# Both attentions that run between the expert picks: masks level with the scores, reciprocals two steps later, turning and weighing later, the meta columns in the shares' bank

## The chip, the cores and the metric

The kernel runs on one core of a Trainium2 chip, in fp32. The metric is the device time of one launch in microseconds. Five engines work side by side, each through its own list of instructions in order, and wait for each other on semaphores: PE (TensorE, matmuls; PEld are its weight loads), DVE (VectorE), ACT (ScalarE), POOL (GpSimd, which here issues the gathers) and SP (which here issues the loads of weights).

## The reference

Two blocks over 256 tokens of width 1024. The first is a layer of RWKV-7 time mixing and a layer of MoBA attention (with 256 tokens one block, so plain causal attention, 16 heads of 64). The second puts 16 meta tokens in front and computes

```
xr, gr, cq, ckv, kr, g_rnn, g_att = split(norm(h) @ w_in)
y_rnn = (rg_lru(conv(xr)) * gelu(gr)) @ w_rnn_out
y_att = mla_attention(...)  # 16 heads, key = 64 + 32 rotary columns, 272 keys
h = h + (sigmoid(g_rnn) * y_rnn + sigmoid(g_att) * y_att) @ w_out
h = h + peer(norm(h))       # experts
```

`peer` scores 2 x 128 keys for each of 8 heads, takes the best 16 of the 256 candidate sums, and reads for each token, head and pick a row of u and a row of v (1024 floats each) from a table of 16,384: `coef = softmax(score) * gelu(u . x)`, `out += coef * v`. With 128 tokens on the partitions that makes 2 halves x 8 heads x 16 = 256 picks, and each brings 128 rows of 8 KB, 1 MB.

## The kernel before

Tokens are cut into two halves of 128 (t = 0 and t = 1). Half 0 goes first through the whole network. At the time when its picks begin, half 1 stands at the MoBA attention; the rest of its way (the "front") is put between the picks of half 0. Picks 0 to 127 belong to half 0, picks 128 to 255 to half 1.

**A pick.** POOL issues the gather into a seat as soon as the pick that sat there before has been used (L3434). There are 7 seats for the first picks, 6 for picks 32 to 45 and 7 again up to pick 109; from pick 110 on there are more. DVE multiplies the u half of the seat with x and sums (L3390, called the dot below), and then runs a few instructions of the routing of a later head (L3274 to L3308). For a pair of picks ACT makes the gelu and the coefficient (L3219, L3223, L3228) and writes one small diagonal matrix for each (L3235). PE multiplies the diagonals with the v halves (L3095, eight records for a pair), which frees both seats.

**The front** is a generator for each engine. It yields either a number, which is paid from a credit of 2 for each pick on PE, or a name and a lag. PE notes in `g.at` at which pick each key was issued; ACT and DVE run the next piece when that pick plus the lag has come. PE stands 3 picks ahead in its count, ACT 2, DVE 0 (`SKEW`): the front's piece of pick n stands on PE before the weighted rows of pick n - 3, and on DVE, with a lag of 1, before the dot of pick n + 1. PE serves picks in pairs, so the pieces of an odd n and of n + 1 both stand before the pair that begins with n - 3. The order on each engine is therefore written out when the program is built, and nothing is chosen on the chip.

**The late pass** (MoBA, half 1) has one step for each pick from -7 to 17. Step i on PE: scores of head i (L1636), transpose of the shares of head i - 6 (L1644), and for even i >= 10 two heads weighed with V (L1656). DVE: mask and row maximum (L1865), factor (L1868), one pick later, and the reciprocal (L1874) and the division (L1875) of the head before. ACT: exponential (L1778) and the copy of the transposed shares (L1789). Both halves of the output share bank 2, so the weighing of head 8 waits until DVE has taken the first half (`late_gated(0)`, L1915).

**The steps** (MLA, half 1) are built alike, from pick 60 to 85: scores (L2172, two banks in turn), transposes (L2182), the 16 meta columns of four heads gathered into a matrix (L2462), transposed in a bank of their own (L2191) and copied (L2475), weighing (L2208, L2214) into bank 2, which DVE clears for every four heads (L2697). DVE masks (L2676) and makes the reciprocal (L2690); ACT negates the maximum (L2446), takes the exponential (L2448), divides (L2454) and copies transposed shares (L2469). Six rows of scores are kept.

Between the two passes stand the projections of half 1 (L2057 and others, "panels" of 8 matmuls, 512 KB of weights each), the convolution on DVE (L2614, L2616), and `gates_in` (L2140), which waits on PE for it:

```
            pe.wait_ge(rgw_loaded.handle, 32)
            for n in range(2):
                pe.wait_ge(convolved[1].handle, convolved[1].at(n + 1))
                gates_in(1, n)
                yield 1.0
```

## Time and profile before

| | |
|---|---|
| runs without a profile | 1435.55 us median of 3 (1432.18 to 1435.96) |
| profiled execution | 1431.92 us, its span 1430.1 us |
| granted TensorE clock, mean | 0.914 |
| busy: PE, DVE, ACT, POOL | 83%, 62%, 36%, 21% |
| moved by DMA | 426.47 MB, mean 298 GB/s |

The span is the time from the first to the last instruction; 1.8 us lie around it. Busy shares are means over stages with different limits, so they say little of any one stage. The picks run from 604 us to the end. Before that the gathers play no part.

### The profile page before, as it was taken

The numbers are of one execution on the slowest core, as the hardware profiler recorded it, in microseconds if no ns is written. First come the engines' busy times: TensorE is split into PE (matmuls) and PEld (weight loads), VectorE is DVE, ScalarE is ACT, GpSimd is POOL, SyncE is SP. The second block draws the span as 40 slices with busy tenths as digits, with TensorE's granted clock in tenths as the row PEclk, the third lists the DMA queues.
The fourth block names the chain that finished last, engine by engine and source line by source line (L and its number), as shares of the span: only waits on it lengthen the run. The fifth ranks groups of instructions, "written<-read, shape, count | busy, mean of one in ns | idle before, by whom it ended". The sixth has DMA issues, their size and how long they took to land.

```text
span 1430.1 us, 23324 instructions
## 1 busy us (share of the span) xinstructions
PE 1183.0 (83%) x8780; PEld 798.2 (56%) x8780; DVE 884.5 (62%) x2297; ACT 515.9 (36%) x1538; POOL 294.7 (21%) x277
## 2 busy tenths in 40 slices
PE   7999998999999999986888987888766676576554
PEld 4446788986689989852666864457433222222111
DVE  7527876546534541588556636765369787777654
ACT  1215223121431530244334534842253434344334
POOL 0000000000000000124221213332253444444440
PEclk9999999999999999968989999999978867878777
DMA  8444100343566867868998999899999999999996
GB/s 311 155 155 134 33 4 3 118 147 122 191 228 226 293 236 249 299 279 351 417 383 327 409 388 418 314 398 421 418 424 424 423 426 424 426 426 424 425 426 254
DMA packets 85984, 426.47 MB, mean 298 GB/s; under 512 B 11183, under 2 KB 15663, under 8 KB 52657
## 3 DMA queue, kind: packets, MB, share of 16 engines
q0 software_dynamic: 38304, 273.70, 46.5%
q1 hardware_dynamic: 47426, 151.03, 29.3%
q8 instruction: 70, 1.15, 0.3%
q14 instruction: 40, 0.33, 0.1%
q10 hardware_dynamic: 144, 0.26, 0.0%
HBM read 421.80 MB, written 3.15 MB: 297 GB/s over the span
## 4 chain that ended last, share of the span: by engine, by line
PE 45%; DMA 27%; DVE 8%; ACT 4%; issue 3%; POOL 2%; POOLq 0%; DVEq 0%; ACTq 0%
DMA cst<-peer_in,arena 16%; PE bank L2057 13%; PE bank L3095 6%; DMA ring<-stream_in 5%; DMA arena<-peer_in,arena 5%; PE bank L1441 3%; PE bank L1528 2%; PE bank L1494 2%; DVE arena L3390 2%; PE bank L847 2%; PE bank L646 1%; PE bank L656 1%; PE bank L2982 1%; DVE cst L3390 1%; PE bank L1671 1%
## 5 line engine op out<-in xcount | busy, mean ns | idle before, releaser
L3095 PE MATMUL bank<-arena 128*64 128x512 f32 x808 | 268.5, 751 | 132.7 <-ACT arena L3235 132.7
L3390 DVE CUSTOM_DVE_ANT_0 arena<-arena 128x1024 f32<-128x1024 f32 x202 | 246.2, 1224 | 140.5 <-DMA arena<-peer_in,arena 137.7
L3434 POOL DMA_INDIRECT arena<-peer_in,arena x202 | 226.2, 1120 | 422.5 <-PE bank L3095 353.6
L2057 PE MATMUL bank<-arena,ring 128*128 128x128 f32 (+1 forms) x2112 | 249.6, 278 | 16.2 <-DMA ring<-stream_in 15.5
L2057 PEld LDWEIGHTS bank<-arena,ring 128*128 128x128 f32 x2112 | 242.2, 192 | 31.9 <-issue 23.1
L3095 PEld LDWEIGHTS bank<-arena 128*64 128x64 f32 x808 | 68.1, 160 | 269.0 <-issue 265.2
L3219 ACT ACTIVATE arena<-arena 128x2 f32<-128x2 f32 (+1 forms) x130 | 26.4, 203 | 390.5 <-DVE arena L3390 390.5
L3095 PE MATMUL bank<-row,arena 128*64 128x512 f32 x112 | 65.1, 712 | 28.3 <-ACT arena L3235 28.2
L3228 ACT ACTIVATE arena<-arena 128x1 f32<-128x1 f32 x256 | 84.2, 375 | 8.3 <-DVE arena L3396 7.5
L3223 ACT ACTIVATE arena<-arena 128x1 f32<-128x1 f32 x256 | 85.4, 380 | 4.3
L2982 PEld LDWEIGHTS bank<-arena,ring 128*128 128x128 f32 x512 | 62.8, 201 | 27.5 <-issue 27.5
L3235 ACT ACTIVATE arena<-cst,arena 128x64 f32<-128x64 f32 x256 | 76.3, 334 | 0.2
L3095 PE MATMUL bank<-cst,arena 128*64 128x512 f32 x104 | 66.3, 772 | 5.3 <-ACT arena L3235 5.3
L2982 PE MATMUL bank<-arena,ring 128*128 128x128 f32 x512 | 67.9, 289 | 0.0
L497 PE MATMUL bank<-ring,arena 128*128 128x512 f32 x128 | 55.1, 592 | 0.0
L1948 POOL DMA_DIRECT2D spill<-arena x2 | 1.1, 536 | 249.1 <-DVE arena L1839 249.1
L1441 PE MATMUL bank<-arena,ring 128*128 128x256 f32 x224 | 49.5, 379 | 0.0
L1441 PEld LDWEIGHTS bank<-arena,ring 128*128 128x128 f32 x224 | 42.5, 190 | 8.3 <-issue 2.9
L3390 DVE CUSTOM_DVE_ANT_0 cst<-cst,arena 128x1024 f32<-128x1024 f32 x26 | 31.9, 1225 | 24.4 <-DMA cst<-peer_in,arena 24.3
L3095 PEld LDWEIGHTS bank<-row,arena 128*64 128x64 f32 x112 | 14.8, 152 | 55.9 <-issue 55.6
L1826 DVE RECIPROCAL arena<-arena 128x512 f32<-128x512 f32 x8 | 26.8, 3353 | 29.6 <-ACT arena L1725 29.6
L3434 POOL DMA_INDIRECT row<-peer_in,arena x28 | 30.9, 1103 | 68.2 <-PE bank L3095 64.5
(412 smaller groups left out, 1870.2 us busy)
## 6 DMA issues: line engine op xcount, KB each, us to landing
ring<-stream_in SPq DMA_DIRECT2D x255, 512.0 KB, 5.9
ring<-stream_in SPq DMA_DIRECT2D x16, 384.0 KB, 8.2
arena<-peer_in,arena POOLq DMA_INDIRECT x202, 20.5
row<-rows_in SPq DMA_DIRECT2D x4, 512.0 KB, 18.4
spill<-arena POOLq DMA_DIRECT2D x4, 512.0 KB, 5.5
cst<-rg_w_in SPq DMA_DIRECT2D x2, 1024.0 KB, 8.6
ring<-stream_in SPq DMA_DIRECT2D x16, 128.0 KB, 4.1
arena<-spill POOLq DMA_DIRECT2D x4, 512.0 KB, 7.7
```

What stands on the lines that cost most here:

```text
L497: mm = nc.tensor.matmul(banks[t][:, :], mix[name][:, k, t * P:(t + 1) * P], slot[:, i * 512:(i + 1) * 512], start=k == 0, stop=k == KT - 1)
L847: mm = nc.tensor.matmul(bank, slot[:, k * P:(k + 1) * P], kT[:, k, t * P:(t + 1) * P], start=k == 0, stop=k == KT - 1)
L1441: mm = nc.tensor.matmul(bank[:, (m % 2) * T:(m % 2 + 1) * T], slot[:, k * P:(k + 1) * P], src[:, k, :], start=k == 0, stop=k == KT - 1)
L1494: mm = nc.tensor.matmul(core.banks[core.bank_at["vb", t, half][0]][:, :], xn["kb"][:, k, t * P:(t + 1) * P], slot[:, i * 512:(i + 1) * 512 ...
L2057: mm = nc.tensor.matmul(bank[:, at:at + width], slot[:, first + k * cols:first + (k + 1) * cols], src[:, k, :], start=k == 0, stop=k == kt ...
L2982: mm = nc.tensor.matmul(bank[:, i * P:(i + 1) * P], slot[:, k * P:(k + 1) * P], n2[t][:, k, :], start=k == 0, stop=k == KT - 1)
L3095: return nc.tensor.matmul(core.banks[2 * t + b][rows_of(j), :], diag[i % ND], places[seat[i]][:, D + b * 512:D + (b + 1) * 512], start=Fal ...
L3223: nc.scalar.activation(act_out[:, i:i + 1], act_out[:, i:i + 1], ACT.Tanh, bias=steep, scale=steep).then_inc(*activated.up())
L3228: nc.scalar.activation(act_out[:, i:i + 1], act_out[:, i:i + 1], ACT.Identity, bias=share, scale=share).then_inc(*coef_ready.up())
L3235: nc.scalar.activation(diag[i % ND], cst("halves"), ACT.Copy, scale=act_out[:, i:i + 1])\
L3390: ins = nc.vector.tensor_tensor_reduce(out=row, in0=row, in1=X2[t][i % 2], scale=STEEP, scalar=0.0, op0=ALU.mult, op1=ALU.add, accum_out=d ...
L3434: pool.indirect_dma_start(out=places[seat[i]], out_offset=None, in_=g.names["peer"], in_offset=bass.IndirectOffsetOnAxis(ap=index[:, i:i + ...
```

## The change

In the late pass DVE masks a head at the pick at which PE issues its scores (lag 0 where it was 1) and does the reciprocal and the division 3 steps after the mask where it was 1, so two steps later against the masks and one pick later in the program. ACT copies transposed shares one step later. `late_gated(0)` stays at step 16, which lag 0 puts one pick earlier. The output projection waits 3 picks after the last step where it waited 4; as each later piece of the front hangs on the one before, all of the front behind it stands one pick earlier.

In the steps the masks get lag 0 as well (`q2` gets lag 2 where it had 1, so the rotations stay where they were), reciprocals come 3 steps after the mask where it was 1, ACT divides 5 steps after the scores where it was 3 and copies shares 8 after where it was 6; PE turns 7 after where it was 6 and weighs 11 after where it was 10. Eight rows of scores are kept where it was six. The meta columns are transposed into the third quarter of the bank of the fourth head's shares and no longer into a bank of their own, so that `turn_meta`, its claim and its wait go; ACT still copies them by an instruction of their own.

```diff
@@ moba, PE and ACT
-            yield ("late", H + 8), 4
+            yield ("late", H + 8), 3
...
-                if 6 <= i < H + 6:
-                    late_keep(i - 6)
+                if 7 <= i < H + 7:
+                    late_keep(i - 7)
@@ moba, DVE
             for i in range(H + 9):
-                yield ("late", i), 1
+                yield ("late", i), 0
                 if i < H:
                     mask(i, 1)
-                if 1 <= i < H + 1:
-                    divide(i - 1, 1)
+                if 3 <= i < H + 3:
+                    divide(i - 3, 1)
                 if i == 16:
                     late_gated(0)
@@ second_mix
-    HELD, ROWS = (H, 4), (H, 6)
+    HELD, ROWS = (H, 4), (H, 8)
...
+        if t and n >= 6:
+            return LOW[:, (n - 6) * S:(n - 5) * S]
@@ second_mix, PE
+            if t and h % 4 == 3:
+                pe.wait_ge(meta_laid[t].handle, meta_laid[t].at(h + 1))
+                mm = nc.tensor.transpose(bank[:, 2 * P:3 * P], META_P[t][h // 4 % 2], cst("ident"))
...
-                if 6 <= i < H + 6:
-                    turn(i - 6, 1, 6 + i % 2)
-                if 6 <= i < H + 6 and (i - 6) % 4 == 3:
-                    turn_meta((i - 6) // 4, 1, 4)
-                if i >= 10 and i % 2 == 0:
-                    weigh((i - 10) // 2, 1, 2)
+                if 7 <= i < H + 7:
+                    turn(i - 7, 1, 6 + (i - 7) % 2)
+                if i >= 11 and i % 2:
+                    weigh((i - 11) // 2, 1, 2)
@@ second_mix, ACT
-                if 6 <= i < H + 6:
-                    keep(i - 6, 1)
+                if 8 <= i < H + 8:
+                    keep(i - 8, 1)
                 if 2 <= i < H + 2:
                     exps(i - 2, 1)
-                if 3 <= i < H + 3:
-                    divide(i - 3, 1)
-                    lay_meta(i - 3, 1)
+                if 5 <= i < H + 5:
+                    divide(i - 5, 1)
+                    lay_meta(i - 5, 1)
@@ second_mix, DVE
-                yield ("q2", n, 1), 1
+                yield ("q2", n, 1), 2
...
-                yield ("step", i), 1
+                yield ("step", i), 0
                 if i < H:
                     mask(i, 1)
-                if 1 <= i < H + 1:
-                    divide(i - 1, 1)
-                if i >= 12 and i % 4 == 0:
-                    keep_out((i - 12) // 4, 1)
+                if 3 <= i < H + 3:
+                    divide(i - 3, 1)
+                if i >= 13 and i % 4 == 1:
+                    keep_out((i - 13) // 4, 1)
```

The lines of the changed kernel lie 10 further down around the picks (the dot is L3400 for L3390, the weighted rows L3105 for L3095) and 2 further at the projections (L2059, L2142).

**First place, DVE at the end of the late pass**, around picks 9 and 10. L1874 and L1875 are reciprocal and division, L1915 is `late_gated`, the large ISA row of L3390 is the dot of a pick. Before:

```order
L3396 TENSOR_TENSOR arena<-arena 128x2
L3274 MAX arena<-arena 128x8
L3276 MAX_INDEX arena<-arena 128x8
L3277 MATCH_REPLACE cst<-arena 128x128
L3279 MAX arena<-cst 128x8
L3281 MAX_INDEX arena<-arena,cst 128x8
L3289 CAST arena<-arena 128x16
L3274 MAX arena<-arena 128x8
L1874 RECIPROCAL small<-small 128x1
L1875 TENSOR_SCALAR arena<-arena,small 128x256
L1915 TENSOR_TENSOR arena<-bank,arena 128x512
L3390 ISA arena<-arena 128x1024
```

and of the changed kernel, where the two dots shown first and last are those of picks 8 and 9:

```order
L3400 ISA arena<-arena 128x1024
L3400 ISA arena 128x1
L1874 RECIPROCAL small<-small 128x1
L1875 TENSOR_SCALAR arena<-arena,small 128x256
L1915 TENSOR_TENSOR arena<-bank,arena 128x512
L3400 ISA arena<-arena 128x1024
L3400 ISA arena 128x1
L3406 TENSOR_TENSOR arena<-arena 128x2
L3284 MAX arena<-arena 128x8
L3286 MAX_INDEX arena<-arena 128x8
```

The reading of bank 2 (L1915) stood before the dot of pick 10, behind the routing pieces of the pair 8 and 9; now it stands before the dot of pick 9, ahead of them.

**Second place, PE at `gates_in`** (L2140, changed kernel L2142), between the weighted rows of picks 30 to 37. The rows with `row` in them are those of picks 32 and 33, the x4 behind them picks 34 and 35. Before:

```order
L3095 MATMUL bank<-arena 64x512
L3095 MATMUL bank<-row,arena 64x512
L2057 MATMUL bank<-arena,ring 128x128 x32
L3095 MATMUL bank<-arena 64x512 x4
L2982 MATMUL bank<-arena,ring 128x128 x8
L2140 MATMUL bank<-arena,cst 128x128 x16
L2079 MATMUL bank<-arena,ring 128x128 x8
L2057 MATMUL bank<-arena,ring 128x128 x8
L3095 MATMUL bank<-arena 64x512 x4
```

and of the changed kernel:

```order
L3105 MATMUL bank<-arena 64x512
L3105 MATMUL bank<-row,arena 64x512
L2059 MATMUL bank<-arena,ring 128x128 x16
L2142 MATMUL bank<-arena,cst 128x128 x16
L3105 MATMUL bank<-arena 64x512 x4
L2992 MATMUL bank<-arena,ring 128x128 x8
L2081 MATMUL bank<-arena,ring 128x128 x8
L2059 MATMUL bank<-arena,ring 128x128 x24
L3105 MATMUL bank<-arena 64x512 x4
```

`gates_in` stood behind the weighted rows of picks 34 and 35 and before those of 36 and 37; now it stands before those of 34 and 35.

**Third place, DVE at the convolution** that `gates_in` waits for (L2614 and L2616; changed kernel L2624 and L2626). The dot with `row` in it is that of pick 39. Before:

```order
L3390 ISA arena 128x1
L2614 TENSOR_SCALAR arena<-arena,vec 128x128 x4
L2616 SCALAR_TENSOR_TENSOR arena<-arena,vec 128x128 x4
L3390 ISA row,arena<-row,arena 128x1024
L3390 ISA arena 128x1
L3396 TENSOR_TENSOR arena<-arena 128x2
L3274 MAX arena<-cst 128x8
L3276 MAX_INDEX arena<-arena,cst 128x8
L3277 MATCH_REPLACE cst<-arena,cst 128x256
L3279 MAX arena<-cst 128x8
L2616 SCALAR_TENSOR_TENSOR arena<-arena,vec 128x128 x8
L3390 ISA arena<-arena 128x1024
```

and of the changed kernel:

```order
L2624 TENSOR_SCALAR arena<-arena,vec 128x128 x4
L2626 SCALAR_TENSOR_TENSOR arena<-arena,vec 128x128 x4
L3400 ISA arena<-arena 128x1024
L3400 ISA arena 128x1
L2626 SCALAR_TENSOR_TENSOR arena<-arena,vec 128x128 x8
L3400 ISA row,arena<-row,arena 128x1024
L3400 ISA arena 128x1
L3406 TENSOR_TENSOR arena<-arena 128x2
L3284 MAX arena<-cst 128x8
L3286 MAX_INDEX arena<-arena,cst 128x8
L3287 MATCH_REPLACE cst<-arena,cst 128x256
L3289 MAX arena<-cst 128x8
```

The last eight convolution instructions stood between the dots of picks 39 and 40; now they stand between those of 38 and 39, one pick earlier, while PE waits for them two picks earlier.

## Rows read from the trace of the kernel before

**Rows 1.** The page: span, then DMA share and GB/s in 40 slices.

```profile
span 1430.1 us, 23324 instructions
...
DMA  8444100343566867868998999899999999999996
GB/s 311 155 155 134 33 4 3 118 147 122 191 228 226 293 236 249 299 279 351 417 383 327 409 388 418 314 398 421 418 424 424 423 426 424 426 426 424 425 426 254
```

**Rows 2.** Busy us of each engine by stretch, clock, DMA share, GB/s.

```profile
core 0: us, PE busy (x) PEld busy (x) DVE busy (x) ACT busy (x) POOL busy (x), PEclk, DMA share, GB/s
610.00:680.00 70.00, 52.76 (x256) 28.01 (x255) 59.35 (x199) 30.71 (x113) 21.04 (x18) 0.77 0.79 313
680.00:870.00 190.00, 167.32 (x1201) 131.53 (x1198) 111.22 (x306) 74.75 (x207) 45.06 (x39) 0.95 0.96 386
870.00:950.00 80.00, 59.61 (x340) 33.89 (x339) 56.30 (x181) 52.30 (x194) 29.84 (x26) 0.89 0.92 363
950.00:1060.00 110.00, 85.80 (x604) 60.86 (x603) 56.87 (x144) 38.42 (x125) 36.74 (x36) 0.92 1.02 421
1060.00:1430.10 370.10, 232.43 (x832) 83.96 (x832) 273.90 (x736) 153.03 (x548) 147.22 (x134) 0.79 0.97 408
```

**Rows 3.** Waits from 604 to 674 us: total, times, longest.

```profile
ACT arena L1789 <- PE bank L1656: 11.1, 5, 4.9
...
DVE small L1874 <- ACT arena L1778: 7.2, 8, 1.8
...
PE bank L1636 <- DVE small L1865: 6.4, 6, 1.9
PE bank L1656 <- DVE arena L1915: 5.3, 1, 5.3
```

**Rows 4.** The same columns as rows 2, two slices of the late pass.

```profile
620.00:630.00 10.00, 8.38 (x27) 4.34 (x28) 7.87 (x33) 3.64 (x13) 0.00 (x0) 0.50 0.41 172
...
660.00:670.00 10.00, 8.73 (x66) 5.15 (x64) 9.17 (x26) 3.97 (x16) 6.70 (x5) 1.00 0.71 270
```

**Rows 5.** Waits from 870 to 950 us.

```profile
PE bank L2172 <- DVE small L2676: 12.6, 8, 3.5
...
DVE small L2690 <- ACT arena L2448: 11.7, 14, 2.0
...
PE bank L2208 <- DVE arena L2697: 3.3, 3, 2.4
```

**Rows 6.** DVE in order of time: the dots of picks 64 and 78.

```profile
889.23 1.21 DVE L3390 CUSTOM_DVE_ANT_0 arena<-arena 128x1024 f32<-128x1024 f32 x1
...
934.53 1.22 DVE L3390 CUSTOM_DVE_ANT_0 arena<-arena 128x1024 f32<-128x1024 f32 x1
```

**Rows 7.** ACT in order of time: first instruction of two pairs, one after the other.

```profile
906.40 0.20 ACT L3219 ACTIVATE arena<-arena 128x2 f32<-128x2 f32 x1 [0.69 <-DVE arena L3390]
...
912.79 0.20 ACT L3219 ACTIVATE arena<-arena 128x2 f32<-128x2 f32 x1 [0.68 <-DVE arena L3390]
```

**Rows 8.** PE in order of time: picks 34 and 35, gates, picks 36 and 37, four panels.

```profile
753.49 1.94 PE L3095 MATMUL bank<-arena 128*64 128x512 f32 x8
755.36 2.05 PE L2982 MATMUL bank<-arena,ring 128*128 128x128 f32 x16
757.25 1.95 PE L2140 MATMUL bank<-arena,cst 128*128 128x128 f32 x16
765.50 3.46 PE L2140 MATMUL bank<-arena,cst 128*128 128x128 f32 x16 [6.30 <-DVE arena L2616]
...
772.47 1.94 PE L3095 MATMUL bank<-arena 128*64 128x512 f32 x8
...
774.33 7.41 PE L2057 MATMUL bank<-arena,ring 128*128 128x128 f32 x64
```

**Rows 9.** DVE in order of time: dot of pick 38, convolution pieces.

```profile
756.08 1.23 DVE L3390 CUSTOM_DVE_ANT_0 arena<-arena 128x1024 f32<-128x1024 f32 x1 [1.23 <-DMA arena<-peer_in,arena]
...
763.13 2.31 DVE L2616 SCALAR_TENSOR_TENSOR arena<-arena,vec 128x128 f32<-128x128 f32 x8
```

**Rows 10.** The same columns as rows 2, around the gates.

```profile
760.00:770.00 10.00, 4.50 (x27) 4.50 (x28) 7.63 (x24) 6.08 (x23) 0.00 (x0) 0.66 0.69 289
770.00:780.00 10.00, 10.00 (x81) 8.50 (x80) 5.28 (x16) 6.10 (x14) 2.10 (x2) 1.00 0.66 215
```

**Rows 11.** ACT in order of time: a load of a function table.

```profile
720.33 1.28 ACT L3223 ACT_TABLE_LOAD   x1
721.63 0.67 ACT L3223 ACTIVATE arena<-arena 128x1 f32<-128x1 f32 x2
```

More of the change, by code:

```diff
@@ L2211, in weigh @@
             if j % 2:
-                copied(pe, ("pm_c", n, t))
+                if t == 0:
+                    copied(pe, ("pm_c", n, t))
                 for i in range(2):
@@ L2459, in lay_meta @@
             if n >= 2 and h % 4 == 0:
-                filled(act, ("pm_c", n - 2, t))
+                filled(act, ("pt_c", 4 * n - 5, t) if t else ("pm_c", n - 2, t))
             to = META_P[t][n % 2].rearrange("p (d h w) -> p d h w", d=2, w=NM)[:, :, h % 4, :]
@@ L2468, in keep @@
                 act.wait_ge(weighed_out[t].handle, weighed_out[t].at((h - HELD[t]) // 2 + 1))
-            nc.scalar.activation(PT[t][:, at:at + width], bank[:, 0:width], ACT.Copy).then_inc(*free(("pt_c", h, t)))
+            ins = nc.scalar.activation(PT[t][:, at:at + width], bank[:, 0:width], ACT.Copy)
+            if t == 0:
+                ins.then_inc(*free(("pt_c", h, t)))
             if h % 4 == 3:
                 n = h // 4
-                bank = filled(act, ("pm_c", n, t))
+                meta = bank[:, 2 * P:3 * P] if t else filled(act, ("pm_c", n, t))[:, 0:P]
                 if n >= len(PM[t]):
                     filled(act, ("o_c", n - len(PM[t]), t))
-                nc.scalar.activation(PM[t][n % len(PM[t])], bank[:, 0:P], ACT.Copy).then_inc(*free(("pm_c", n, t)))
+                ins = nc.scalar.activation(PM[t][n % len(PM[t])], meta, ACT.Copy)
+                if t == 0:
+                    ins.then_inc(*free(("pm_c", n, t)))
+            if t:
+                ins.then_inc(*free(("pt_c", h, t)))
         def open_attended(t, n):
```

## The prediction

> **What bounds the kernel now.** I read the page first, then a table of stretches, then in each stretch the waits, and last single instructions in order of time. The page's slices of DMA share and GB/s [rows 1] show where the end is decided: from the 20th slice on the DMA engines move some 400 GB/s, and in the last 15 slices nearly always more than 414, so the picks of half 1 wait for bytes. The stretches say the same in numbers: share 1.02 from 950 to 1060 us, 0.97 from there to the end, where the last microseconds move nothing [rows 2]. The bytes are fixed, 426 MB, and the change moves none. So the change is worth what it takes from, or adds to, the time in which DMA stands idle before 950 us. Taking 1.02 as full, that idle time is (1.02 - 0.79) x 70 = 16 us in the late pass, (1.02 - 0.96) x 190 = 11 us in the projections, and (1.02 - 0.92) x 80 = 8 us in the steps [rows 2].
>
> Why is DMA idle there? A gather leaves only when a seat is free, and a seat is freed by the weighted rows on PE, which come behind a dot on DVE, a chain on ACT and whatever of the front stands ahead of them. In the late pass DVE is busy 59.35 of 70 us [rows 2], the most of any engine that the loop needs, and 7.2 us of its idle time stand ahead of the reciprocal, which waits for the exponential of the head masked just before [rows 3]. Behind the waiting reciprocal are queued the division, the next dot and so the next seat. PE has one wait of 5.3 us, for the reading of bank 2 by `late_gated`, just ahead of the weighted rows of picks 8 and 9 [rows 3]; DMA falls to 0.71 in the slice in which these end late [rows 4].
>
> In the steps DVE waits 11.7 us in 14 parts for exponentials [rows 5]. The two engines hand each other the work: the dot of an odd pick starts ACT's chain, behind that chain stands the next exponential, behind the exponential the reciprocal, and behind it the next dot. From the dot of pick 64 to that of pick 78 there are seven pairs in 45.3 us, 6.47 us a pair [rows 6]. ACT's own work in a pair is 912.79 - 906.40 = 6.39 us less an idle 0.68 us, that is 5.71 us [rows 7].
>
> **The change part by part.**
>
> *Late pass, masks and reciprocals.* No instruction is added or taken. The mask of a head comes one pick earlier, its reciprocal one pick later, and the exponential between them stays: two picks lie between where one did. The wait of 7.2 us [rows 3] goes but for remnants; its next owner is DVE's own work. The masks could now wait for PE. PE issues the scores three picks ahead, and from 620 to 630 us it works at the lower of its two clocks, 1.2 GHz (granted 0.50), busy 8.38 of 10 us [rows 4]: there PE can't follow a faster DVE, and of the 7.2 us I leave about 2.2 to it. PE's 6.4 us of waits for a mask [rows 3] shrink with it, being the same time seen from the other side. Gain 5.0 us; bounds: 0 (all goes to PE at 1.2 GHz) and 7.2.
>
> *Late pass, bank 2 and copies.* `late_gated` stands ahead of the dot of pick 9 and no longer of pick 10, so PE's 5.3 us [rows 3] lose at least a dot and the routing pieces behind it. ACT's copy, which waited 11.1 us for PE [rows 3], comes one pick later, when PE is past it. Both are parts of the same loop and I count them as cover for the 5.0 us, not beside it. Without them the gain would stop at about 7.2 - 5.3 = 2 us.
>
> *Steps.* The exponential comes one pick earlier on ACT and the reciprocal stays where it was. The ping-pong is cut, and what is late next is ACT with 5.71 us a pair. At that pace seven pairs save 7 x (6.47 - 5.71) = 5.3 us. The 12.6 us for which PE waits for masks [rows 5] go along with it. ACT gets no less work, except the wait for the meta bank, and its copies stretch over two more steps, so I take 3.5 us. Bounds: 0, and the stretch's 8 us of idle DMA. `turn_meta`'s own bank and wait go; the transposed matrix still costs one transpose and one copy: 0. Two more rows of scores lie in memory that is free by then: 0; if it were not, a mask would wait for a copy. Reading bank 2 one pick earlier takes the 3.3 us of L2208 [rows 5], which is inside the 3.5.
>
> *Projections, one pick earlier.* Here the change isn't only a shift. Since PE serves pairs, `gates_in` moves from ahead of picks 36 and 37 to ahead of 34 and 35, two picks, while the convolution that it waits for moves by one, from behind the dot of pick 39 to behind that of pick 38. Before, PE waited 6.30 us [rows 8]. Now the weighted rows of 34 and 35 (753.49 before [rows 8]) stand behind that wait. Pick 38 can only come after picks 32 and 33 free their seats, so its dot stays near 756.08 + 1.23 us; then 2.31 us of convolution [rows 9], about 760, and 3.46 us for the second gates [rows 8], about 763.5. Those weighted rows so end near 765.5, ten microseconds late. Behind them come 2.05 us of a query and 7.41 us of four panels [rows 8]: picks 36 and 37 start at 775.0 where they started at 772.47, 2.5 us late. DMA was already idle there, at 0.69 and 0.66 [rows 10], so the delay of picks 34 and 35 replaces a hole with an earlier one, and I count the 2.5 us as loss. Bounds: -1.2 us (PE has then done two panels more, 3.7 us by half of 7.41) and +10.
>
> *Table loads.* ACT loads one function table less, since two pieces that need a square root now follow each other. A load takes 1.28 us and the next activation begins right behind it [rows 11]. ACT waits for dots in the projections, so: 0, at best 1.28 us. The Trainium skill, ScalarE: Activation LUTs, section What ACT_TABLE_LOAD costs, gives about 1283 ns for the load and another 1380 ns of drain, 2.66 us in all; by it the sum would be 1.4 us lower at most. The load's duration agrees with the row, and the row shows no drain behind it.
>
> *The rest one pick earlier* is worth nothing: from 950 us DMA is full [rows 2].
>
> Sum: -5.0 - 3.5 + 2.5 = -6.0 us. Against the profiled execution, 1431.92 us, that is 1425.9. The median of the three plain runs is 3.6 us above that execution, so I put it at 1435.5 - 6.0 = 1429.5 us.
>
> **Rivals.**
> - *Both loops shorten, the gates cost a little* (forecast): 1424 to 1434 us. Chance 0.50.
> - *Given back.* The late pass gains 3 us and the steps 1.5, because landing gathers become the wait, and the gates cost 4.5. For it: DMA share is already 0.96 and 0.92 in the two later stretches [rows 2], so little room is left. Against it: no dot of the late pass waits for DMA among its larger waits [rows 3]. Time 1435.5. Chance 0.26. The Trainium skill, Trainium Kernel Development and Optimization, section Key Constraints, says that transfers of all queues run on the same 16 engines and interleave; by it an earlier gather only takes the turn of a weight panel. The trace agrees where the share is 1.02 and not in the late pass.
> - *Slower, by the gates.* The weighted rows of picks 34 and 35 stand behind a dot that needs the only seats just refilled, and all six run empty. If the hole in DMA grows by the whole ten microseconds and the two loops give 5 together, the time is 1435.5 + 10 - 5 = 1440.5. It decides from a loss of 8.5 us on. Against it: most of that hole is there already [rows 10]. Chance 0.12.
> - *More.* The late pass gives 7.2, the steps 5.3 and the gates -1.2: 13.7 us, 1422. For it: DVE's waits are 7.2 and 11.7 us [rows 3, 5]. Against it: 1.2 GHz on PE, and ACT. Chance 0.12.
>
> **How the numbers follow.** About 0.3% (4.3 us) is what a measurement of this kernel tells from no change. Below 1431.2 lie 0.43 of the forecast and all of the last case: faster 0.55. Within: 0.07 and 0.22 of the second case, 0.29. Slower: 0.12 and 0.04, 0.16. The range 1420 to 1438 leaves out the far end of the last case, 0.05, and most of the slower one with a tail of the second, 0.13. The forecast's own range is 1424 to 1434.
>
> **What would show it.** Right, if DVE's idle time ahead of the late reciprocal falls under 2 us, the share from 610 us to the end of the late pass rises above 0.83, the steps take 6 us a pair with hardly a wait at L2690's successor, and PE's long wait at the gates stands ahead of picks 34 and 35. Wrong, if masks wait for PE in the place of the reciprocals, if dots begin to wait for landings so that the pair stays at 6.4 us, or if picks 36 and 37 start more than 8 us behind their place.

## The result, and the profile after

The changed kernel takes **1419.37 us** (median of 4 runs, 1416.69 to 1421.12) against 1433.87 for the kernel before on the same chip (4 runs, 1431.59 to 1435.96): ratio **0.9898, interval 0.987 to 0.9925**, faster by 14.5 us. A second comparison, e9_after below, gave 0.9882. The forecast had -6.0 us and 1429.5; its range ended at 1420. The sign was right, the forecast size less than half of the measured one.

The profiled execution of the changed kernel took 1421.12 us, the slowest of its four, so the two traces differ by 10.8 us where the medians differ by 14.5.

The page, with the same rows as [rows 1]:

```profile
span 1419.3 us, 23316 instructions
...
DMA  8443100343556876879998999899999999999995
GB/s 308 155 156 141 34 3 3 120 141 127 193 195 229 301 256 229 296 294 403 421 421 337 418 365 423 340 381 419 422 424 424 423 424 426 426 425 426 425 425 242
```

The stretches of [rows 2], now of the changed kernel:

```profile
core 0: us, PE busy (x) PEld busy (x) DVE busy (x) ACT busy (x) POOL busy (x), PEclk, DMA share, GB/s
610.00:680.00 70.00, 61.50 (x346) 36.91 (x345) 63.22 (x219) 32.43 (x123) 21.72 (x20) 0.84 0.88 356
680.00:870.00 190.00, 164.86 (x1146) 127.14 (x1144) 111.54 (x302) 73.86 (x209) 43.36 (x40) 0.93 0.97 394
870.00:950.00 80.00, 63.18 (x376) 36.44 (x373) 60.38 (x192) 53.35 (x199) 26.89 (x25) 0.90 0.94 369
950.00:1060.00 110.00, 86.94 (x582) 58.75 (x581) 58.67 (x153) 37.78 (x124) 42.85 (x39) 0.91 1.02 421
```

The reader is to see the second last number: 0.79 to 0.88, 0.96 to 0.97, 0.92 to 0.94. Taking 1.02 as full again, DMA idles (1.02 - 0.88) x 70 + (1.02 - 0.97) x 190 + (1.02 - 0.94) x 80 = 25.7 us, where it was 35: 9 us less, nearly the 10.8 us between the traces. A share has two digits, which leaves some 2 us open on either side; within that the way the prediction kept its books holds.

The waits of the late pass, 604 to 674 us (compare [rows 3]):

```profile
PE bank L1644 <- ACT arena L1789: 5.1, 4, 2.4
...
DVE arena L1865 <- PE bank L1636: 2.1, 3, 1.3
...
PE bank L1636 <- DVE small L1865: 1.9, 1, 1.9
```

DVE's 7.2 us ahead of the late reciprocal are gone altogether. Masks now wait 2.1 us for PE, and PE waits 5.1 us for ACT's copies.

The waits of the steps, 861 to 941 us (compare [rows 5]; L2686 is the mask, L2174 the scores, L2184 the turn of a head's shares, L2473 their copy):

```profile
PE bank L2174 <- DVE small L2686: 7.8, 3, 5.0
DVE row L3400 <- DMA row<-peer_in,arena: 7.5, 2, 5.5
DVE arena L3400 <- DMA arena<-peer_in,arena: 6.0, 6, 2.4
PE bank L2184 <- ACT arena L2473: 6.0, 7, 1.5
```

And the dots of picks 64 and 78 (compare [rows 6]):

```profile
878.02 1.23 DVE L3400 CUSTOM_DVE_ANT_0 arena<-arena 128x1024 f32<-128x1024 f32 x1 [0.33 <-DMA arena<-peer_in,arena]
...
918.12 1.23 DVE L3400 CUSTOM_DVE_ANT_0 arena<-arena 128x1024 f32<-128x1024 f32 x1 [0.45 <-DMA arena<-peer_in,arena]
```

Seven pairs in 40.1 us, 5.73 us a pair, where it was 6.47. No reciprocal waits for an exponential any more; most of what DVE waits for are landings: the two rows above and 2.0 us for seats in `cst`, 15.5 us together, where it was 11.1 us from 870 to 950 us before.

The gates on PE (compare [rows 8]), and the stretch around them:

```profile
739.69 2.02 PE L2142 MATMUL bank<-arena,cst 128*128 128x128 f32 x16 [0.94 <-issue]
748.48 3.78 PE L2142 MATMUL bank<-arena,cst 128*128 128x128 f32 x16 [6.76 <-DVE arena L2626]
752.19 1.94 PE L3105 MATMUL bank<-arena 128*64 128x512 f32 x8
```
```profile
750.00:760.00 10.00, 10.00 (x72) 8.39 (x72) 4.81 (x16) 8.00 (x21) 2.83 (x2) 0.89 0.44 161
```

The weighted rows of picks 34 and 35 stand behind the wait, as forecast. So all four signs that the prediction had named for being right were there, and its sum was still far too small: they tell where the gain comes from and not how large it is.

The next table is worked out from the traces: the start of the weighted rows of a pick, less that of the kernel before, in us. The kernels of the columns are those of the experiments.

| pick | changed | e1_shift | e3_late | e4_steps | e2_noshift | e10_bank | e13_own | e17 |
|---|---|---|---|---|---|---|---|---|
| 0 | -5.0 | +1.2 | -5.1 | +7.5 | -3.5 | +0.6 | -2.9 | -6.1 |
| 16 | -5.7 | +9.0 | -7.3 | +7.2 | -5.8 | +1.1 | -2.8 | -6.7 |
| 34 | -1.3 | +11.5 | -7.4 | +6.6 | -7.9 | +0.6 | +0.6 | -7.0 |
| 36 | -9.3 | +4.7 | -6.8 | +7.8 | -6.5 | +2.3 | -7.3 | -11.8 |
| 54 | -11.8 | +2.5 | -4.3 | +9.7 | -5.8 | +4.2 | -9.8 | -13.1 |
| 78 | -14.3 | +8.0 | -6.6 | +2.4 | -12.8 | 0.0 | -5.4 | -19.0 |
| 84 | -5.4 | +15.4 | -6.6 | +2.4 | -12.7 | +0.1 | +1.0 | -19.0 |
| 104 | -13.6 | +6.5 | -6.9 | +0.3 | -17.8 | -0.8 | -7.9 | -22.1 |
| 254 | -11.9 | +9.2 | -6.1 | +0.3 | -14.3 | +0.1 | -5.3 | -20.3 |

A column is one execution. The +7.5 at pick 0 of e4_steps arose before any pick, and its time (1433.39 us) was 8 us over the highest of its six others; what that column tells is the fall from +9.7 to +0.3 behind it.

### The profile page after: what moved, and what is told of

Its sections match the earlier page's. It is cut to its first block, busy times and chain, and to the rows that moved or that the text cites. A ratio compares the mean times of both kernels' runs of the same rounds, so it can differ in the third digit from the quotient of the medians.

```text
span 1419.3 us, 23316 instructions
## 1 busy us (share of the span) xinstructions
PE 1181.3 (83%) x8780; PEld 797.2 (56%) x8780; DVE 885.3 (62%) x2297; ACT 513.6 (36%) x1537; POOL 291.2 (21%) x277
## 4 chain that ended last, share of the span: by engine, by line
PE 46%; DMA 24%; DVE 11%; ACT 4%; issue 3%; POOL 2%; POOLq 0%; DVEq 0%; ACTq 0%
PE bank L2059 14%; DMA arena<-peer_in,arena 13%; DMA cst<-peer_in,arena 9%; PE bank L3105 7%; PE bank L1441 3%; DVE arena L3400 3%; DMA ring<-stream_in 2%; PE bank L1528 2%; PE bank L1494 2%; PE bank L847 2%; PE bank L2992 2%; PE bank L646 1%; PE bank L656 1%; PE bank L1671 1%; PE bank L1574 1%
## 5 line engine op out<-in xcount | busy, mean ns | idle before, releaser
L3105 PE MATMUL bank<-arena 128*64 128x512 f32 x808 | 266.5, 745 | 132.3 <-ACT arena L3245 132.3
L3400 DVE CUSTOM_DVE_ANT_0 arena<-arena 128x1024 f32<-128x1024 f32 x202 | 246.3, 1224 | 141.3 <-DMA arena<-peer_in,arena 138.4
L3444 POOL DMA_INDIRECT arena<-peer_in,arena x202 | 223.0, 1104 | 419.4 <-PE bank L3105 349.5
L2059 PEld LDWEIGHTS bank<-arena,ring 128*128 128x128 f32 x2112 | 242.9, 192 | 17.8 <-issue 14.5
L2059 PE MATMUL bank<-arena,ring 128*128 128x128 f32 (+1 forms) x2112 | 248.6, 278 | 1.5 <-DMA ring<-stream_in 0.8
L3105 PEld LDWEIGHTS bank<-arena 128*64 128x64 f32 x808 | 67.2, 157 | 268.1 <-issue 265.1
L3105 PE MATMUL bank<-row,arena 128*64 128x512 f32 x112 | 69.2, 751 | 31.3 <-ACT arena L3245 31.3
L3105 PE MATMUL bank<-cst,arena 128*64 128x512 f32 x104 | 63.7, 745 | 0.3 <-ACT arena L3245 0.3
L3400 DVE CUSTOM_DVE_ANT_0 cst<-cst,arena 128x1024 f32<-128x1024 f32 x26 | 31.8, 1224 | 29.2 <-DMA cst<-peer_in,arena 29.1
L3400 DVE CUSTOM_DVE_ANT_0 row<-row,arena 128x1024 f32<-128x1024 f32 x28 | 34.3, 1224 | 24.9 <-DMA row<-peer_in,arena 24.6
L3105 PEld LDWEIGHTS bank<-row,arena 128*64 128x64 f32 x112 | 15.8, 162 | 58.8 <-issue 58.3
```

The lines of the kernel that those rows point to most:

```text
L2059: mm = nc.tensor.matmul(bank[:, at:at + width], slot[:, first + k * cols:first + (k + 1) * cols], src[:, k, :], start=k == 0, stop=k == kt ...
L3105: return nc.tensor.matmul(core.banks[2 * t + b][rows_of(j), :], diag[i % ND], places[seat[i]][:, D + b * 512:D + (b + 1) * 512], start=Fal ...
L3400: ins = nc.vector.tensor_tensor_reduce(out=row, in0=row, in1=X2[t][i % 2], scale=STEEP, scalar=0.0, op0=ALU.mult, op1=ALU.add, accum_out=d ...
L3444: pool.indirect_dma_start(out=places[seat[i]], out_offset=None, in_=g.names["peer"], in_offset=bass.IndirectOffsetOnAxis(ap=index[:, i:i + ...
```

## The experiments

All times are beside the kernel before on the same chip, whose median was between 1433.1 and 1435.5 us in the five groups of runs. Intervals are of the ratio and span 2 to 6 us to either side; gains given in us below are the difference of the two medians of one group.

| run | what it is | ratio, interval | us |
|---|---|---|---|
| e1_shift | before + shift | 1.0042, 1.002 to 1.0064 | 1438.98 |
| e3_late | before + late pass | 0.9945, 0.9927 to 0.9964 | 1425.53 |
| e4_steps | before + steps | 0.9921, 0.9892 to 0.995 | 1423.15 |
| e2_noshift, e18_noshift | changed, without shift | 0.9915 and 0.9905 | 1421.40, 1421.16 |
| e5_q2 | before + rotations a pick later | 0.9981, 0.9957 to 1.0005 | 1431.11 |
| e6_noq2 | before + steps, rotations as before | 0.9929, 0.9903 to 0.9955 | 1424.93 |
| e7_ownbank | before + steps, meta bank kept | 0.9968, 0.9949 to 0.9987 | 1429.89 |
| e10_bank | before + shared bank | 0.9974, 0.9946 to 1.0002 | 1430.89 |
| e9_after | changed, again | 0.9882, 0.9844 to 0.9921 | 1420.25 |
| e11_recip | changed, reciprocals 2 steps behind | 0.992, 0.989 to 0.995 | 1424.23 |
| e13_own | changed, meta bank kept | 0.9953, 0.9937 to 0.9969 | 1426.78 |
| e15_gated | changed, `late_gated` a pick later | 0.9901, 0.9874 to 0.9928 | 1420.99 |
| e8_conv, e14_conv | changed, convolutions earlier | 0.9878 and 0.9896 | 1415.16, 1418.84 |
| e12_conv2 | changed, all four taps earlier | 0.9879, 0.9841 to 0.9918 | 1420.29 |
| e16, e17_conv_noshift | e14 without shift | 0.9862 and 0.9869 | 1414.11, 1415.14 |

**The change in three parts.** The shift alone, the late pass alone and the steps alone, each laid on the kernel before, and the whole without the shift. The late pass and the steps are the hunks of the diff above for them; with the steps go the rotations two picks behind, which the shift needs as well. The shift is one number:

```
-            yield ("late", H + 8), 4
+            yield ("late", H + 8), 3
```

> The kernel before, with only the output projection waiting 3 picks for 4 after the late pass, so that all of the front behind it stands one pick earlier (and the rotations of the queries keep their place by a lag of 2). Theory A (placement): the shift pays by itself, because the first two panels of the output projection fill a wait of PE ahead of picks 16 and 17 and the rest follows; less 2 us for the gates. Expected 3 to 5 us under the kernel before, ratio 0.997. Theory B (as in the prediction): the shift only costs what the gates cost, 2.5 us over the kernel before, ratio 1.002.

> The changed kernel with the output projection put back to a wait of 4 picks: every part of the change but the shift. Theory A: 3 to 5 us slower than the changed kernel, about 10 us under the kernel before, ratio 0.993, and gates_in stands behind picks 34 and 35 again. Theory B: 2.5 us faster than the changed kernel, about 17 under the kernel before, ratio 0.988.

> The kernel before with the late pass of the changed one alone (masks level with the scores, reciprocals three steps after, copies one step later), no shift and the old steps. Both theories: DVE's wait ahead of the late reciprocal nearly gone, picks 16 and 17 used 6 to 7 us earlier than before. A: of these 6 us are left at the end, ratio 0.996. Rival: the late pass explains most of the 14.5 us by itself, ratio 0.992 or less.

> The kernel before with the steps of the changed one alone (masks, reciprocals, copies, turning, weighing, eight rows, meta columns in the shares' bank, rotations with a lag of 2), no shift and the old late pass. Both theories: 2 to 3.5 us under the kernel before, ratio 0.998, the pair of picks at about 6 us for 6.47. Rival (given back): the steps end earlier, the gathers land no earlier and the time is that of before, ratio 1.000.

Measured: +5.5 us, -12.0, -7.9 and -10.3. A theory that the shift itself pays falls: alone it costs. The three parts add to -12.7 us, and the whole gave -14.5 and -15.2. Late pass and steps together without the shift gave -12, less than the -18.2 of their sum: perhaps some of the one gain is had in place of the other, but with 3 to 4 us to either side of each of the three numbers, that isn't shown.

In e3_late the late pass alone shows this:

```profile
610.00:680.00 70.00, 54.76 (x314) 31.97 (x313) 64.89 (x221) 33.54 (x125) 20.19 (x20) 0.89 0.92 365
```
```profile
DVE arena L1865 <- PE bank L1636: 1.1, 3, 0.6
DVE small L1874 <- ACT arena L1778: 0.2, 1, 0.2
```

The first fence is the stretch of the late pass with the columns of [rows 2], the second all that DVE waited for from 604 to 674 us: 7.2 us of waiting for exponentials became 0.2, and no more than 1.1 came back as masks that wait for PE. The DMA share rose from 0.79 to 0.92.

**What in the steps pays?** They gave 10 us where I had put 3.5. First the rotations: alone, and taken out of the steps' part.

```
             for n in range(4):
-                yield ("q2", n, 1), 1
+                yield ("q2", n, 1), 2
                 rotate_queries(1, n)
```

> The kernel before with one number changed: the four rotations of the second queries (rotate_queries(n, 1)) stand on DVE two picks behind the piece of PE that they read, not one. The steps' part of the change alone took about 10 us off (0.9921), where the prediction had 3.5 and nothing for the rotations. Theory Q: about half of that comes from here, because DVE no longer stands 12.7 us ahead of the dot of pick 56, waiting for ACT's copy of the turned queries; then this kernel takes 3 to 6 us off, ratio 0.996 to 0.998. Theory P, that the cut hand-over between DVE and ACT in the steps carries the whole: 0 to 1 us, ratio 0.999 to 1.001, since the gain of the dot of pick 56 frees no seat sooner.

> The steps' part of the change alone, as in the run e4_steps, but with the rotations left where the kernel before has them (one pick behind). Theory P (the hand-over between DVE and ACT): still 8 to 10 us off, ratio 0.993 to 0.9945, and pairs of picks 64 to 78 at 6 us or below. Theory Q (the rotations): 4 to 6 us off, ratio 0.9955 to 0.997.

Measured: -3.6 us with an interval that holds no change, and -9.8 without them. The steps' gain is the same with and without within the measurement, so theory Q falls as the main cause. The pace that theory P expected, 6 us a pair or below, is missed in the trace of e6_noq2: 6.49. That execution is the highest of its seven (1437.81 us, 13 over the median), and 4.1 us of it are one wait of DVE ahead of the dot of pick 78; up to pick 76 it is 6.17, where the kernel before has 6.69 and e4_steps 5.74. So the pace there is cut by less than P said. In the trace of e5_q2 the dot of pick 56 comes 15.1 us sooner and its weighted rows 0.7 us later: a dot that is early frees no seat by itself.

Then the bank. `turn_meta` gets its own bank back, once in the new order of the steps, and the shared bank is tried in the old order.

```
                     turn(i - 7, 1, 6 + (i - 7) % 2)
+                    if (i - 7) % 4 == 3:
+                        turn_meta((i - 7) // 4, 1, 5)
...
-            if t and h % 4 == 3:
-                pe.wait_ge(meta_laid[t].handle, meta_laid[t].at(h + 1))
-                mm = nc.tensor.transpose(bank[:, 2 * P:3 * P], META_P[t][h // 4 % 2], cst("ident"))
```

> The steps' part of the change alone, as in e4_steps, but the meta columns are still turned into a bank of their own (a bank of the scores, as before, now the other one of the two) by their own piece, and copied and freed as before. If the shared bank is worth nothing, as the prediction has it: the same as e4_steps, ratio 0.990 to 0.994. Rival: PE's wait for a scores' bank that both a mask and a copy must leave is part of the steps' gain; then 3 us or more are missing, ratio 0.9945 or above.

> The kernel before, with one thing of the steps' part alone: the meta columns are turned in the bank of the shares and copied with them, in the old order of the steps. The run with a bank of their own in the new order (e7_ownbank) missed about half of the steps' gain. Theory: the bank matters only in the new order, where the copy that frees a scores' bank comes a step later; in the old one PE waits 0.7 us for it, so 0 to 1 us here, ratio 0.999 to 1.001. Rival: the shared bank gains by itself what was missing, 4 to 6 us, ratio 0.996 to 0.9975.

> The changed kernel with the meta columns of the steps turned into a bank of their own again (the other of the two scores' banks), by their own piece, copied and freed as before; all else as changed. Theory B: the shared bank is about half of the steps' gain in the new order, since PE's next scores otherwise wait for the copy that frees the scores' bank (9.7 us of such waits on the matmuls and their loads together when the steps' part ran with a bank of its own): 4 to 6 us of the gain are lost, ratio 0.992 to 0.994. Rival, the prediction's own price of nothing: 0.988 to 0.990.

Measured: -4.8 us in e7_ownbank, where e4_steps had -10.3; -4.6 in e10_bank with an interval that just holds no change; and in e13_own -7.8 us, so that undoing the bank in the changed kernel loses about 7 us, with intervals that stand apart (0.9937 to 0.9969 against 0.987 to 0.9925). The price of nothing is refuted, for the new order. For the old order the median of e10_bank lies where the rival put it (0.9974) and not where my theory did. Its trace says the same, if read like the column of e4_steps: 4.2 us behind the kernel before at pick 54, level from pick 78 on, so 4.2 us gained between. The shared bank may thus be worth some 4 us in the old order too, where PE waited 0.7 us for the copy and 1.9 us ahead of `turn_meta`; with no change still in the interval, that stays open. Both runs with a bank of their own use the other of the two scores' banks, at a place in the new order that was chosen for them; another place, or a free bank, was not tried. PE's waits in e13_own, 861 to 941 us (L2477 is the copy of the turned meta columns there, L2678 the mask):

```profile
PE bank L2174 <- ACT arena L2477: 10.1, 2, 5.1
PE bank L2174 <- DVE small L2678: 7.8, 3, 4.8
```

The changed kernel has the second row (7.8 us) and not the first. In its place it has 4.4 us for the same copy at the weighing (L2213 behind L2481), ahead of the weighted rows of picks 80 and 81, and all of PE's waits from 861 to 941 us come to 21.7 us against 23.1: the price of the bank is read from the times, not from the 10.1 us. The meta columns stood in a bank of the scores. A step after them PE wants that bank for the next scores, and ACT's copy, which frees it, now comes a step later in the order. In the table e13_own is 2.1 us behind the changed kernel at pick 0, 2.0 at pick 54, and 8.9 at pick 78. Its pair from pick 64 to 78 takes 7.00 us, that of e7_ownbank 6.35 and that of e4_steps 5.94, where the changed kernel has 5.73. These are single executions, and e6_noq2 has 6.49 with the bank shared, so a pace alone doesn't show what the bank is worth.

Two parts of the steps' change were not run alone: the eight rows of scores and the later copies.

**How far must the reciprocal stand behind?** Two steps and not three, in both loops:

```
-                if 3 <= i < H + 3:
-                    divide(i - 3, 1)
+                if 2 <= i < H + 2:
+                    divide(i - 2, 1)
```

> The changed kernel with the reciprocals of both attentions two steps behind the masks and not three, so that each stands at the dot where it stood before the change, relative to its head; all else as changed. Theory P (the gain is that of the cut hand-over): the masks alone already open one pick of room, but the exponential's chain again ends last in some steps; DVE waits 5 us or more for exponentials again over both loops, and 4 to 8 us of the gain are lost, ratio 0.992 to 0.996. Rival: one pick of room is enough, and the third step is worth nothing: 0.989 to 0.991, with hardly a wait.

Measured: 0.992, 4.0 us above e9_after in the same group of runs. DVE's waits in the steps (861 to 941 us), then in the late pass (604 to 674 us):

```profile
DVE small L2700 <- ACT arena L2452: 8.2, 12, 2.0
```
```profile
DVE small L1874 <- ACT arena L1778: 2.5, 3, 1.8
```

10.7 of the 18.9 us of [rows 3, 5] are back. The intervals of the two runs overlap (0.989 to 0.995, 0.9844 to 0.9921), so the waits are shown and their price of 4 us is likely.

**Is the earlier `late_gated` what lets the late pass gain?**

```
-                if i == 16:
+                if i == 17:
                     late_gated(0)
```

> The changed kernel with late_gated(0) a pick later on DVE, ahead of pick 10 and not of pick 9, where it stood before the change. The prediction counted its earlier place as cover for the 5.0 us of the late pass, without which the gain there would stop at about 2 us. If so, PE's wait for the reading of bank 2 grows back to some 4 us and 3 us or more of the whole gain are lost: ratio 0.991 to 0.993. Rival: the late pass gains by the cut hand-over alone, and later the delay of picks 8 and 9 is made up: 0.988 to 0.990.

Measured: 0.9901, 1420.99 us, where the rival put it; the interval (0.9874 to 0.9928) doesn't exclude a loss of 3 us. PE waits for the reading of bank 2 again, but for little, and not for the 4 us that were expected:

```profile
PE bank L1656 <- DVE arena L1915: 1.3, 1, 1.3
```

**The gates and the shift.** The convolutions of half 1 a pick earlier, with the shift and without, and once all four taps together:

```
-                yield ("xr", part, 1), 3
+                yield ("xr", part, 1), 2
                 convolve(1, part, 0)
                 convolve(1, part, 1)
-                yield ("xr", part, 1), 4
+                yield ("xr", part, 1), 3
```

> The changed kernel with the convolutions of half 1 one pick earlier on DVE (two and three picks behind their piece, not three and four), so that PE's gates meet a convolution that is done, or nearly. In the changed kernel the weighted rows of picks 34 and 35 come about 10 us late there, and the DMA share is 0.44 in the 10 us around it. If that hole costs bytes (the prediction's loss of 2.5 us, or more): 3 to 6 us faster than the changed kernel, ratio to the kernel before 0.986 to 0.988. Rival: the hole is only moved, since the seats run empty a little later at the next wait, and the time is that of the changed kernel, 0.989 to 0.991. A convolution that is earlier can also make DVE wait for PE and hold back a dot: then 0.992 or above.

> The changed kernel once more, unaltered, beside the runs below on the same chip. If the first comparison holds, 0.987 to 0.9925 of the kernel before; the sum of the parts run one by one (-7.9 us for the late pass, -10.3 for the steps, +5.5 for the shift: -12.7 us, 0.991) lies in the same interval, so a result there would say that the parts simply add. Below 0.986 or above 0.993 they would not.

> The changed kernel with the convolutions of half 1 earlier still: all four taps of a part two picks behind its piece. With three of them a pick earlier (e8_conv) the time was 0.9878, 3.2 us of PE's wait at the gates were left, and DVE's last taps stood behind a dot and its routing pieces. If those 3.2 us still cost: another 1 to 3 us, ratio 0.986 to 0.988. Rival: the block of 4.6 us on DVE holds up a dot and gives it back: 0.988 to 0.990.

> The changed kernel with the convolutions of half 1 a pick earlier, the same kernel as e8_conv (0.9878 there, when the changed kernel, in two other comparisons, had 0.9898 and 0.9882). If the gates' wait costs the changed kernel some 3 us, this one lies at 0.986 to 0.988 again; if it costs nothing, at 0.988 to 0.990.

> The kernel of e14_conv without the shift (the projections start one pick later again, as before the change). The shift cost 5.5 us when it was made alone, and nothing, or a gain of 2, on top of the rest. If its cost is that of the gates' wait, it has none here and both kernels are the same, 0.986 to 0.989. If the shift gains by itself (one pick more of DMA work done before it is full), this one is 2 to 3 us slower, 0.988 to 0.991; if it costs, 2 to 3 us faster, 0.984 to 0.986.

> The kernel of e16_conv_noshift once more (0.9862 there, against 0.9896 for the same with the shift). If the shift does cost 3 to 5 us even when the gates' wait is small, it lies at 0.985 to 0.988 again; if the difference was that of two single comparisons, at 0.988 to 0.991.

> The changed kernel without the shift, the same as e2_noshift (0.9915 there), beside the run above, which differs from it by the earlier convolutions alone. If the gates' wait costs 3 us or more where nothing is shifted, this one lies 0.002 or more above it, at 0.990 to 0.993; if not, the two are the same within 0.002.

With the shift, earlier convolutions did not separate from the changed kernel: 0.9878 and 0.9896 against 0.9898 and 0.9882; all four taps at once gave 0.9879. Without the shift they gave 0.9862 and 0.9869 against 0.9915 and 0.9905, 6.0 us in the same group of runs. The intervals of that pair overlap (0.9838 to 0.99, 0.9875 to 0.9935), but the gain came twice. The gates in e18_noshift, then in e17_conv_noshift, with the stretch around them behind each:

```profile
753.07 1.95 PE L2142 MATMUL bank<-arena,cst 128*128 128x128 f32 x16
761.71 3.78 PE L2142 MATMUL bank<-arena,cst 128*128 128x128 f32 x16 [6.68 <-DVE arena L2626]
```
```profile
760.00:770.00 10.00, 8.29 (x50) 8.18 (x52) 7.70 (x22) 4.07 (x16) 0.00 (x0) 0.66 0.39 150
```
```profile
750.30 1.95 PE L2142 MATMUL bank<-arena,cst 128*128 128x128 f32 x16
752.68 2.05 PE L2142 MATMUL bank<-arena,cst 128*128 128x128 f32 x16 [0.43 <-DVE arena L2626]
```
```profile
760.00:770.00 10.00, 10.00 (x81) 8.38 (x81) 6.44 (x18) 6.37 (x15) 2.59 (x2) 1.00 0.84 302
```

The wait of 6.68 us is 0.43, the gates behind it take 2.05 us and not 3.78, and DMA is at 0.84 there and not at 0.39. That is the fastest kernel of the study: 1414.11 and 1415.14 us, 1.3% under the kernel before and 4 to 6 us under the changed one.

The shift itself costs 5.5 us alone. In company it gains: 14.5 and 15.2 us under the kernel before with it, 12.0 and 11.9 without, so 2.9 us. With early convolutions it costs 1.6 us (19.6 and 15.7 with, 20.4 and 18.0 without). The last two are within what these runs can tell. Why it costs alone is not settled. The traces show two places where the shifted kernels lag. One is picks 34 and 35, behind the gates. The other is picks 82 to 88: at pick 84 the changed kernel is 7.3 us behind e2_noshift, at pick 78 it was 1.5 us ahead, and e1_shift loses 7.4 us between the two. There the shift takes PE's pieces across the border of a pair once more. Ahead of the weighted rows of pick 82 stand 64 matmuls of the front in both shifted kernels and 32 in the others, 3.7 us more, and the lag shrinks by 5.9 us at pick 90, ahead of which none stand in place of 32. In the changed kernel the 4.4 us for the copy of the meta columns come on top, which e2_noshift doesn't have. The DMA share from 870 to 950 us is 0.99 in e2_noshift and e18_noshift, and 0.94 and 0.96 in the two traces of the changed kernel.

## Why the prediction came out too small

**Where the time is lost: right.** DMA idle before 950 us fell by 9 us and the trace by 10.8; from 950 to 1060 us the share is 1.02 and behind that 0.97, both as before.

**Late pass, -5.0: mechanism right, size low.** Measured -7.9 (interval -5.2 to -10.5). The step that failed is "of the 7.2 us I leave about 2.2 to it", PE at its lower clock. Masks waited 1.1 us for PE in e3_late. The stretch of the late pass (610 to 680 us) was granted 0.89 there and not 0.77. The traces with the old late pass have 0.70 to 0.81 in it, seven in all, those with the new one 0.83 to 0.89, but for e18_noshift with 0.76. So PE spent less of the stretch at 1.2 GHz, and the row of the slow clock from which I took the 2.2 us did not hold for the changed order. That PE keeps the higher clock because it waits less is my reading; no run separates it.

**"Without them the gain would stop at about 7.2 - 5.3 = 2 us": not borne out.** With `late_gated` back in its place, PE's wait was 1.3 us, not 5.3, and the median was 0.7 to 1.6 us above those of the changed kernel, with some 4 us to either side. Why so little of it comes back wasn't tried, nor were the copies put back. The copies did not become cover either: PE waits 5.1 us for them now, and the pass is faster all the same.

**Steps, -3.5: the term that failed.** It measured -10.3 and, without the rotations, -9.8. Three steps of it failed:
- "`turn_meta`'s own bank and wait go; the transposed matrix still costs one transpose and one copy: 0." I counted instructions and not the bank. It is a bank of the scores, and in e13_own PE waits for it twice, 10.1 us (4.3 in e7_ownbank). Leaving it out is worth 5 to 7 us: the difference of e4_steps and e7_ownbank, and of e13_own and the changed kernel. My "0" compared with the 0.7 us that the old order lost there, and the change moved the copy that frees the bank a step back at the same time.
- "what is late next is ACT with 5.71 us a pair", seven pairs, 5.3 us. The pair takes 5.73, but that was luck. The 5.71 us hold a second idle of 0.30 us (ACT waits for PE ahead of 910.32), so the work was 5.41. In the 40.1 us of the changed kernel ACT is busy 33.2 us, 4.74 a pair, and DVE 34.4, so neither was busy throughout; e14_conv has 5.59 us a pair, below the 5.71. With a bank of its own for the meta columns the pair takes 6.35 (e7_ownbank) and 7.00 (e13_own), so the 4.8 us of e7_ownbank are not the 5.3 us of this pace, though they lie near it. Nor does the shared bank make the pace by itself: the trace of e6_noq2 has it and 6.49.
- The sum counted pairs from pick 64 on. In the traces of e4_steps and e7_ownbank 4.0 us come earlier, between picks 54 and 60, nearly all at one wait of PE for a mask ahead of the weighted rows of pick 58. The mask is level with the scores now, and the wait is gone. The kernel before, then e4_steps:

```profile
876.07 0.73 PE L2172 MATMUL bank<-arena 128*128 128x144 f32 x4 [3.52 <-DVE small L2676]
```
```profile
881.65 1.10 PE L2174 MATMUL bank<-arena 128*128 128x144 f32 x8
```

The prediction let the 12.6 us for which PE waits for masks "go along with it" and gave them no term. How much of the 4.0 us is left at the end no run shows.

The cut from 5.3 to 3.5 us, because ACT's "copies stretch over two more steps", had a reason: PE waits 6.0 us for these copies in the changed kernel (L2184 behind L2473), where it had none of them among its waits before. What that costs isn't shown either.

**Projections, +2.5: place right, price not shown.** The weighted rows of picks 34 and 35 moved by +9.6 and +9.9 us against those of pick 32 (e1_shift, changed), picks 36 and 37 by +2.8 and +1.9: the "ten microseconds late" and "2.5 us late" of the text. What it costs in time is 5.5 alone and between -2.9 and +1.6 in company. The text took the hole as fixed since it was there before; e16 and e17_conv_noshift show that the hole, in its old place, could be closed, and their medians put 6 to 8 us on it.

**Table load, 0: not told apart.** Between 690 and 960 us there are eight loads where there were nine. The Trainium skill (ScalarE: Activation LUTs, What ACT_TABLE_LOAD costs) has a drain behind each load; here again the next activation starts right behind it. Columns: start, duration.

```profile
711.03 1.28 ACT L3233 ACT_TABLE_LOAD   x1
712.33 0.67 ACT L3233 ACTIVATE arena<-arena 128x1 f32<-128x1 f32 x2
```

**"Given back": it did not come.** The argument was that landings become the wait. They did: 15.5 us of DVE's waits in the steps are for landings. But there were 11.1 before, and DMA, at 0.94 where it was 0.92, moved more and still wasn't full. In e4_steps the share of 870 to 950 us rose to 0.99. The Trainium skill (Trainium Kernel Development and Optimization, Key Constraints) says that transfers of all queues interleave on the same engines; by the prediction's reading an earlier gather then takes a panel's turn. That can only be so when the engines are full, and here their mean share was below 1.02, so there was room.

## What to carry to other kernels

When two engines hand each other the work in a loop, the pace of the slower one is to be had only if nothing else holds the loop: here the pair took 5.59 to 6.49 us in the traces with the bank shared, 6.35 and 7.00 in those without, where 5.71 had been put down as ACT's own. Count the first steps of a loop too; 4.0 us lay there. When an order is changed, list each buffer with who frees it in the new order: PE waited 0.7 us for a copy before, and 4.3 and 10.1 us for the same copy a step later. A wait that stands in the old and the new trace alike (here the gates, 6.3 and 6.8 us) may be the best thing left to mend.

## What was not expected of the hardware

A wait of PE can cost more than its length. Behind 6.68 us of waiting the same 16 gates took 3.78 us (granted 0.50 from 761.70 to 765.30 us), behind 0.43 us of it 2.05 (granted 1.00). In the changed kernel the granted clock right behind the waits of 6.76 us and of 4.45 us (ahead of L2213, 929.58 to 934.03) was half, the 1.2 GHz level (second and first row):

```profile
934.00:940.00 6.00, 5.97 (x21) 2.60 (x22) 5.29 (x16) 2.03 (x8) 0.00 (x0) 0.51 1.01 422
748.00:752.00 4.00, 3.52 (x16) 3.49 (x16) 3.38 (x11) 2.37 (x10) 0.00 (x0) 0.50 0.57 228
```

The weighted rows at 936 us took 1.06 us each for two side by side; where PE had not waited so long, in e2_noshift, 0.59. The length of one wait doesn't decide it alone: in the changed kernel the rows at 912.49 us took 1.06 us too (granted 0.51) behind two waits of 1.51 us, and in e17_conv_noshift the matmuls behind a wait of 2.13 us ran at their 2.05 us. The first row also shows that a slow PE need not cost bytes: DMA is at 1.01 through it.
